# One-hot gate products in split fp32r, twelve dot products in the second table stage, and residual transposes in a one-core decoder block

## The reference

```python
q = (xt @ w_q).reshape(T, PEER_HEADS, 2, PEER_DK_HALF)
s = einsum('thpd,hpnd->thpn', q, sub_keys)
s1, i1 = top_k(s[:, :, 0], 16);  s2, i2 = top_k(s[:, :, 1], 16)
top_s, pos = top_k(s1[..., :, None] + s2[..., None, :], 16)      # idx = i1 * 128 + i2
gates = softmax(top_s)
y[t] = sum over heads and experts e of  gates[t,e] * gelu(u[e] . x[t]) * v[e]
return rms_norm(h + y)
```

## Time and profile before

| | us |
|---|---|
| median of 3 runs | 1690.25 (1688.8 to 1690.59) |
| time of the profiled execution | 1690.17 |
| its span, first to last instruction | 1688.4 |
| mixers, merge, queries and scores | up to 528.7 |
| U stage, 128 steps, 96 quads | 528.7 to 1153.65 |
| hand-over to V (three residuals) | 1153.65 to 1158.9 |
| V stage, 128 steps | 1158.9 to 1683.3 |
| final norm and stores | to 1688.4 |

### The profile page before, as it was taken

How to read it: one execution, slowest core, us unless ns; L and a number is a source line. 1 busy time by engine, 2 the same in 40 slices (tenths; PEclk the granted TensorE clock), 3 DMA queues, 4 the chain that set the end, 5 groups by cost and what they waited for, 6 DMA issues and landing times.

```text
span 1688.4 us, 24662 instructions
## 1 busy us (share of the span) xinstructions
PE 1674.1 (99%) x9069; PEld 1477.8 (88%) x9069; DVE 1234.8 (73%) x2291; ACT 780.1 (46%) x1379; POOL 773.8 (46%) x484
## 2 busy tenths in 40 slices
PE   9999999999999999999999999999999999999998
PEld 6788877788888999999999999999888888888887
DVE  7977636744524899999986575744888888888886
ACT  5533326544212343467766767733333333333334
POOL 4545322434334878765555577774222322222220
PEclk9999999999999999999999999999999999999999
DMA  8322432374334899978777699997999999999993
GB/s 224 101 75 63 113 91 60 94 240 140 113 119 146 304 302 328 323 260 308 252 277 256 248 361 363 398 390 246 352 370 350 374 349 371 354 358 364 356 360 124
DMA packets 258639, 433.68 MB, mean 257 GB/s; under 512 B 14736, under 2 KB 181904, under 8 KB 256856
## 3 DMA queue, kind: packets, MB, share of 16 engines
q1 hardware_dynamic: 202648, 249.12, 45.4%
q0 software_dynamic: 36864, 134.23, 21.0%
q10 hardware_dynamic: 19008, 48.77, 7.8%
HBM read 372.82 MB, written 59.24 MB: 256 GB/s over the span
## 4 chain that ended last, share of the span: by engine, by line
PE 58%; DVE 7%; issue 2%; ACT 1%; DMA 0%; POOL 0%; ACTq 0%; DVEq 0%
PE bank L251 17%; PE bank L253 17%; PE bank L252 17%; PE bank L1764 5%; DVE lists L1538 1%; DVE rows L1259 1%; DVE slot L1587 1%; DVE lists L1576 1%; DVE lists L1582 0%; DVE top_i L1536 0%; ACT hot L1441 0%; DVE top_i L1548 0%; DVE pair_i L1548 0%; DMA rows<-in_u_rows,expert 0%; DVE pair_i L1536 0%
## 5 line engine op out<-in xcount | busy, mean ns | idle before, releaser
L246 POOL TENSOR_TENSOR spl_a<-raw,spl_a 128x1024 fp32r<-128x1024 f32 x170 | 409.7, 2412 | 333.9 <-ACT spl_a L242 332.7
L242 ACT ACTIVATE spl_a<-raw 128x1024 fp32r<-128x1024 f32 x296 | 313.1, 1059 | 388.9 <-PE bank L253 383.8
L251 PE MATMUL bank<-act,spl_a 128*128 128x384 f32 (+1 forms) x1216 | 426.2, 351 | 1.8 <-PEq L1181 1.7
L253 PE MATMUL bank<-act,spl_a 128*128 128x384 f32 (+1 forms) x1216 | 418.1, 344 | 0.0
L252 PE MATMUL bank<-act,spl_a 128*128 128x384 f32 (+1 forms) x1216 | 417.7, 344 | 0.0
L251 PE MATMUL bank<-spl_a,aws 128*128 128x512 f32 x768 | 298.9, 389 | 0.0
L253 PE MATMUL bank<-spl_a,aws 128*128 128x512 f32 x768 | 298.8, 389 | 0.0
L252 PE MATMUL bank<-spl_a,aws 128*128 128x512 f32 x768 | 298.8, 389 | 0.0
L1250 POOL DMA_INDIRECT rows<-in_v_tab,expert x128 | 135.1, 1055 | 347.2 <-DVE hot L1656 336.9
L251 PEld LDWEIGHTS bank<-act,spl_a 128*128 128x128 f32 x1216 | 229.1, 188 | 12.3 <-issue 3.6
L252 PEld LDWEIGHTS bank<-act,spl_a 128*128 128x128 f32 x1216 | 229.1, 188 | 7.7 <-issue 0.7
(11 more groups left out here) (316 smaller groups left out, 2386.1 us busy)
## 6 DMA issues: line engine op xcount, KB each, us to landing
raw<-in_u_t SPq DMA_DIRECT2D x128, 512.0 KB, 4.9
raw<-in_v_tab SPq DMA_DIRECT2D x128, 512.0 KB, 7.5
dense_gates<-mixbuf ACTq DMA_DIRECT2D x12, 2048.0 KB, 8.8
mixbuf<-dense_gates SPq DMA_DIRECT2D x32, 768.0 KB, 9.3
gelu_ux<-gl ACTq DMA_DIRECT2D x120, 192.0 KB, 5.5
...
```

What stands on the lines that cost most here:

```text
L242: eng.activation(spl(n, 0, slice(0, W)), raw[:, s, :], ACT.Copy).then_inc(hi_done, 1)
L246: eng.tensor_tensor(spl(n, 1, slice(0, W)), raw[:, n % RAW, :], spl(n, 0, slice(0, W)).bitcast(F32), ALU.subtract).then_inc(lo_done, 1)
L251: nc.tensor.matmul(out, w_hi, x_hi, start=first, stop=False)
L253: return nc.tensor.matmul(out, w_lo, x_hi, start=False, stop=last)
```

## The change

Four things are changed.

1. **Quads in fp32r.** `hot` becomes fp32r. Each fp32 product of two tables becomes two fp32r products with the same first table: with the rounded gate, and with what rounding left of the gate. The second scaled table, `hot_lo`, is made by DVE with one more instruction a quad (128 x 4 x 128, into the columns of `act` that belong to tile TS). `slots_out` makes two instructions more a tile. The quads' steps, `QUAD_AT`, run from 48 to 118, where they ran from 47 to 114.
2. **Twelve dots later.** The last 12 of the 128 dots stand in the first six steps of the V stage, two a step. The v rows are added from step 7 on, 128 in 115 steps, where it was 128 in 122. The gathers (`GATHER_AT`) end at step 125 where they ended at 118, 122 of them in the U stage. The gelu of the dots and tile TS's residual move to the end of V step 6. ACT's first two `weight_hi` stand behind the last U step, where they stood in step 125.
3. **Residual by transposes.** `is_transpose=True` on the residual's matmuls.
4. **Buffers.** `acc` and `square` lie in `ab`, where they lay in `hot`.

```diff
-            GATES_MIX_AT = [119, 122]
+            GATES_MIX_AT = [122, 123]
-            EXP_AT = [18, 39, 61, 87]
-            SLOTS_AT = [None, 41, 63, 92]
+            EXP_AT = [19, 40, 68, 97]
+            SLOTS_AT = [None, 42, 71, 100]
-            ROW_STEPS = 122
+            LATE = 12
+            ROW_AT, ROW_STEPS = 7, 115
...
-                    if j == NC - 3:
-                        act_e.wait_ge(row_used, SLOTS)
-                        act_e.activation(a_row[:, :], z_row[:, :], ACT.Gelu).then_inc(z_gelu, 1)
-                        weight_hi(0)
-                        weight_hi(1)
+                weight_hi(0)
+                weight_hi(1)
...
+                        settle()
+                        low = gate_lo[:, q * QUAD % P:q * QUAD % P + QUAD]
+                        dve.tensor_tensor(hot_lo(q), hot[:, q % HOTS, 1, :, :].bitcast(F32),
+                                          low.unsqueeze(2).to_broadcast([P, QUAD, NK]), ALU.mult).then_inc(hot_ready, 1)
...
                 quads(8)
-                dots(4)
+                dots(2)
                 normalise(NT - 1)
                 dots(2)
                 slots_out(NT - 1)
-                for step in range(16):
-                    quads(2)
+                for step in range(11):
+                    quads(min(3, NQUAD - made[1]))
                     dots(2 + step % 2)
...
+                    if j < LATE // 2:
+                        dots(2)
...
-                            ins = nc.tensor.matmul(bank[4 + q % 2][:, t * P:(t + 1) * P], hot[:, q % HOTS, 0, t, :],
-                                                   hot[:, q % HOTS, 1, t, :], start=True, stop=True)
+                            out = bank[4 + q % 2][:, t * P:(t + 1) * P]
+                            nc.tensor.matmul(out, hot[:, q % HOTS, 0, t, :], hot[:, q % HOTS, 1, t, :],
+                                             start=True, stop=False)
+                            ins = nc.tensor.matmul(out, hot[:, q % HOTS, 0, t, :], hot_lo(q)[:, t, :],
+                                                   start=False, stop=True)
...
-                pe.wait_ge(row_used, SLOTS)
-                residual([x_rows[:, 0, :], x_rows[:, 1, :]], TS, True).then_inc(row_h, 1)
...
+                    if j == ROW_AT - 1:
+                        pe.wait_ge(row_used, SLOTS)
+                        residual([x_rows[:, 0, :], x_rows[:, 1, :]], TS, True).then_inc(row_h, 1)
```

84 lines of the change are left out of this document (50 added, 34 removed), and 19 rows, old and new, of tables (GATHER_AT, QUAD_AT).

## The result

The changed kernel takes 1711.35 us (median of 4 runs, 1708.24 to 1711.89) against 1689.53 for the one before: ratio 1.0126, 95% interval 1.0108 to 1.0143. The forecast was 1689.4 with a range of 1684 to 1700. It was wrong, and so was its sign.

What follows compares the result with a forecast made beforehand. The prediction took PE, busy 99% of the span, to bound the kernel; its terms, -1.2 + 4.4 - 1.6 - 0.6 - 2.3 + 0.5 = -0.8, led from 1690.2 to 1689.4 us, range 1684 to 1700.

Steps and rivals of the forecast that it cites:

- Term 1: Quads' matmuls on PE: 8 fp32r records a quad, each bound by its weight load at 0.110 us; -1.2 us.
- item 1 of "what would show it": Expected sign in the quads: L1787 and L1789 start 0.110 us apart, a quad takes 0.88 us.
- first rival: Quads: load hidden or shortened, columns bound at 0.066 us, 1656 us, or about 1666 if partly hidden; chance 0.11 for both.
- third rival: Quads: an fp32r matmul pays its 13 ns on top of the load; 1698 us, chance 0.09.
- Term 2: DVE's low table in U: net 53 us into 131 us of free DVE time, hidden from PE in general.
- Term 3: Last slots, step 100: PE waits for tk_slots behind DVE's quad 63 and normalise; +4.4 us, 3.5 to 5.
- Term 4: Old PE stalls in U: slots 1 gone (-1.6), quad 24's shrinks (-0.6), the one near quad 57 stays.
- Term 5: Hand-over from U to V: V starts 2.95 us after U's end instead of 5.27; -2.3 us.
- Term 6: First V steps: POOL's lag and two dots a step on DVE barely covered; +0.5 us, from 0 to +5.
- item 4 of "what would show it": Expected sign in V's first eight steps: PE's idle time under 1 us.
- second rival: First V steps: POOL enters V later than reckoned and DVE runs dry; +5.7 with 6 us, 1695 us, chance 0.12.

Runs made afterwards that it cites:

- a3: The changed kernel with DVE's normalise of tile 3 behind six of its eight quads, ahead of all four dots: 1698.2 us.
- a4: a3 with the quads as before the change (fp32 tables, four fp32 products, no low table on DVE): 1696.8 us.
- q1: The changed kernel's fp32r quads and residual transposes on the old schedule and DVE order, no dots moved into V: 1701.2 us.
- b2: The kernel before with the residual by transposes and tile 1's slots at PE step 42 instead of 41: 1683.7 us.
- c2: Probe on a3: the two weight_lo ahead of the V loop replaced by copies of as many PSUM words: 1694.3 us.
- d1: The kernel before with residual transposes, twelve dots and their gathers moved late, rows from V step 7, first two weight_hi behind U: 1691.6 us.

## Why the prediction was wrong, step by step

- **Term 1, the quads (-1.2).** The mechanism was right: the load is the bound, and starts lie 0.111 to 0.112 us apart, as item 1 of "what would show it" asked. But steps with quads are 0.91 to 0.93 us longer for each quad than those without (0.90 before), beyond the 0.90 that the forecast allowed itself: +1.8 us for 96 quads (a3 against a4). The term is off by 3 us: it took a load of 0.110 to be cheaper than an fp32 record of 0.1115, and they are the same; and it had nothing for the matmuls behind the quads, which cost 27 ns a step. The first rival, and with it the 81 ns of the Trainium skill (TensorE: Matmul & The Clock Gate, section Back-to-back issue gap), is refuted for fp32r by the 0.111. The 13 ns of the third rival are there at 256 columns (0.107 + 0.013 = 0.120) and not at 128.
- **Term 2, DVE hidden.** Right for the changed schedule (a4: DVE 67 us lighter and nothing gained but the quads' own 2 us), and q1 prices the cover: without it the fp32r quads cost 16 us instead of 2.
- **Term 3, step 100 (+4.4).** The stall itself measured 4.4 (its lower bound of 3.5 doesn't come out of its own figures, which give 3.9). What failed is that it was taken as the whole price. The step's result is `tk_slots`, and the working asked only who on PE waits for it. SP waits for it as well, in the middle of its queue of unit loads, at its step 96; before, the slots stood at 92, ahead of that. Price: 3.9 us for the second stall and 3.2 for the clock behind it, and 2.4 for the clock at the first: 9.5 us beside the 4.4. This is the largest miss, and one edit (a3) gave 13 us back.
- **Term 4, old stalls (-2.2).** Slots 1: wrong. The forecast let DVE's work come "a step later, 1.7 us at most" and took a whole step for PE; measured, both came 4.2 us later, and the stall of 1.8 is unchanged. b2 shows what a step is worth when nothing else moves. Quad 24's 0.6 went down to 0.3, and the stall of 0.6 near quad 57 stayed, as forecast (at 1000 us).
- **Term 5, the hand-over (-2.3).** 8.9 us instead of 2.95. Of the steps in it, ACT's last gelu began at 1172.05, 4.9 behind U's end instead of 1.2 (+3.6): its splits waited for V table loads, behind gathers that keep the queues full to step 125. ACT's row with its wait:

```profile
1168.75 1.06 ACT L242 ACTIVATE spl_a<-raw 128x1024 fp32r<-128x1024 f32 x1 [7.70 <-DMA raw<-in_v_tab]
```

  And `weight_lo` took 2.97 instead of 0.55 (+2.4), by POOL's splits. 2.95 + 3.6 + 2.4 is the 8.9, but the two can't be had back one by one: in a3 ACT's gelu began 3.0 behind U's end, `weight_lo` then took 4.90, and V started at 8.99 all the same. In both kernels POOL's two splits end 8.3 to 8.4 us behind U and set the start of V; with the splits out of the way (c2) it is 4.83. What failed is the price of `weight_lo(0)`, 0.55 us from a place where POOL splits nothing, and a path that let POOL's lag, reckoned in term 6, reach only DVE's loop. The transposes' own part was right to 0.1 us.
- **Term 6, V's first steps (+0.5).** 1.7 us of waits and 2.8 of low clock. V's first eight steps have no wait of PE, as item 4 of "what would show it" asked; the waits stand at 1213 and 1219, behind 3.5 us in which DVE waited for a reload of the gelu values, a transfer that the forecast did not look at. The second rival (V's start, 1695) named the place and the full queues, but its way, POOL late with its split and DVE's loop behind it, is not what the waits show. d1 costs 6.5 us against the 5.7 of this rival; 1.8 of them are at the hand-over, so that the likeness is luck.
- **The whole.** Against the sum of -0.8, the run gave +21.7 of span. The clock alone is 8.4 of it (2.4, 3.2 and 2.8). No term of the forecast and no rival asked what an idle stretch of PE does to its clock.
